# Projection products spread over attention steps by kind of step: seven shares off the diagonal, four on it

## The reference

```python
h = rmsnorm(x, a_norm)
q, k, v, g = split(h @ w_in, 4)                # w_in: 1024 x 4096
# per head, scale = 1/sqrt(64), strictly causal (s < t):
z = q @ k.T * scale
log_rem = where(mask, log_sigmoid(-z), 0)
after = reverse_cumsum(log_rem) - log_rem      # sum over s < j < t
w = where(mask, exp(log_sigmoid(z) + after), 0)
o = w @ v
y = x + (o * silu(g)) @ w_out
out = rmsnorm(y, final_norm)
```

## Time and profile before

| | |
|---|---|
| median of 3 runs | 1675.85 us (1675.66 to 1677.42) |
| profiled execution, its own time | 1678.26 us |
| its span, first to last instruction | 1676.5 us |
| mean granted TensorE clock | 0.998 |
| busy: PE, PEld, DVE, ACT, POOL | 98%, 82%, 80%, 54%, 14% |
| steps 0 to 599 | 227.8 to 1410.2 us |
| steps 600 to 639 (the last head) | 1410.2 to 1493.3 us |
| chain that ended last | PE 82%, DVE 6%, DMA 5% |

### The profile page before, as it was taken

One profiled execution on the slowest core, in us unless ns is written; L12 is line 12 of the kernel. 1 busy time (PEld: TensorE's weight loads), 2 busy tenths in 40 slices (PEclk: granted clock), 3 DMA queues, 4 the chain that ended last, 5 costly groups with the idle time before them and its releaser, 6 DMA issues.

```text
span 1676.5 us, 23300 instructions
## 1 busy us (share of the span) xinstructions
PE 1650.4 (98%) x8600; PEld 1376.7 (82%) x8600; DVE 1341.2 (80%) x1885; ACT 906.3 (54%) x1779; POOL 234.4 (14%) x212
## 2 busy tenths in 40 slices
PE   8999999999999999999999999999999999999998
PEld 6888878888888888888888888888888888778786
DVE  5435478888898989888888988898889888956765
ACT  6635255655565565656565655666565556651122
POOL 0020012110211011201110211011201110008400
PEclk9999999999999999999999999999999999999999
DMA  9958534252524243334333342425243335398632
GB/s 303 285 153 274 187 120 142 85 151 66 155 75 131 90 127 106 97 102 125 111 91 113 102 138 64 145 76 145 80 122 108 113 95 166 118 357 265 227 141 108
DMA packets 164225, 237.09 MB, mean 141 GB/s; under 512 B 49936, under 2 KB 91920, under 8 KB 164112
## 3 DMA queue, kind: packets, MB, share of 16 engines
q1 hardware_dynamic: 94624, 160.03, 30.4%
q10 hardware_dynamic: 69488, 75.58, 15.1%
HBM read 155.78 MB, written 79.76 MB: 140 GB/s over the span
## 4 chain that ended last, share of the span: by engine, by line
PE 82%; DVE 6%; DMA 5%; ACT 2%; issue 2%; POOL 1%; SPq 1%; ACTq 0%; DVEq 0%
PE proj_ps L737 27%; PE turn_ps L764 13%; PE z_ps L755 7%; PE z_ps L754 7%; PE o_ps L778 7%; PE o_ps L779 7%; PE proj_ps L692 5%; PE o_ps L692 3%; PE turn_ps L692 3%; PE turn_ps L808 2%; DMA gate<-gate_cols 1%; PE z_ps L808 1%; DVE u L1155 1%; DMA wo_raw<-in_w_out 1%; POOL w_raw L668 1%
## 5 line engine op out<-in xcount | busy, mean ns | idle before, releaser
L930 ACT ACTIVATE u<-z_ps 128x512 f32<-128x512 f32 (+3 forms) x640 | 341.8, 534 | 411.0 <-PE z_ps L755 407.5
L1155 DVE TENSOR_TENSOR_SCAN u<-u,u 128x512 f32<-128x512 f32 x384 | 491.0, 1279 | 0.0
L1160 DVE TENSOR_TENSOR r_turned_lo<-turn_ps,r_turned_hi 128x512 fp32r<-128x512 f32 (+3 forms) x640 | 376.5, 588 | 34.8 <-ACT r_turned_hi L936 33.0
L936 ACT ACTIVATE r_turned_hi<-turn_ps 128x512 fp32r<-128x512 f32 (+3 forms) x640 | 340.2, 532 | 60.0 <-issue 44.1
L668 POOL TENSOR_SCALAR w_raw<-w_raw,a_norm_col 128x128 f32<-128x128 f32 x192 | 177.0, 940 | 1202.7 <-DMA w_raw<-in_w_qkg 1202.7
L764 PE MATMUL turn_ps<-ident,u 128*128 128x128 f32 x2176 | 343.1, 273 | 0.1
L737 PE MATMUL proj_ps<-hT_hi,w_hi 128*128 128x512 f32 x768 | 320.2, 417 | 0.0
L737 PE MATMUL proj_ps<-hT_lo,w_hi 128*128 128x512 f32 x768 | 320.0, 417 | 0.0
L737 PE MATMUL proj_ps<-hT_hi,w_lo 128*128 128x512 f32 x768 | 319.8, 416 | 0.0
L764 PEld LDWEIGHTS turn_ps<-ident,u 128*128 128x128 f32 x2176 | 267.8, 140 | 59.3 <-DVE u L1155 0.5
L778 PE MATMUL o_ps<-r_turned_hi,dv_head 128*128 128x512 f32 (+3 forms) x640 | 231.8, 362 | 7.3 <-DVE r_turned_lo L1160 3.1
(11 more groups left out here) (122 smaller groups left out, 1647.8 us busy)
## 6 DMA issues: line engine op xcount, KB each, us to landing
qk_hi_cols<-made_hi ACTq DMA_DIRECT2D x64, 256.0 KB, 2.7
qk_lo_cols<-made_lo ACTq DMA_DIRECT2D x64, 256.0 KB, 3.2
x_T<-in_xT SPq DMA_DIRECT2D x30, 512.0 KB, 5.9
w_raw<-in_w_qkg SPq DMA_DIRECT2D x24, 512.0 KB, 3.4
x_rows<-in_x SPq DMA_DIRECT2D x16, 512.0 KB, 4.6
v_rows<-v_stage ACTq DMA_DIRECT2D x32, 256.0 KB
v_here<-v_rows SPq DMA_DIRECT2D x64, 128.0 KB, 3.1
v_next<-v_rows SPq DMA_DIRECT2D x64, 128.0 KB, 3.2
```

The source lines that it names most:

```text
L930: nc.scalar.activation(u_t[(m // CB) % RU][STEPS[m][3]][:, 0:w], z_ps[m % RZ][:, 0:w], ACT.Sigmoid, scale=-Z_SCALE).then_inc(s_u, 1)
L936: nc.scalar.activation(rt_hi[m % RT][:, 0:w], t_ps[m % RT][:, 0:w], ACT.Copy).then_inc(s_hi, 1)
L1155: nc.vector.tensor_tensor_scan(u, u, other, start, ALU.mult, op).then_inc(s_r, 1)
L1160: nc.vector.tensor_tensor(rt_lo[m % RT][:, 0:w], t_ps[m % RT][:, 0:w], as_f32(rt_hi[m % RT][:, 0:w]), ALU.subtract).then_inc(s_lo, 1)
```

## The change

The products per step are no longer the same for every step. Each off-diagonal step has 7 shares, each diagonal step 4, and a share is 0.5825 product; `SHARES` is the running sum. The totals stay: the last step with products is 636 in both. Steps in which groups end move by up to two; `SHORT_FROM` becomes 603 and the first three of `PIECE_STEP` 607, 611, 615; `WO_FROM` and what lies behind it stay.

```diff
-FILL_NUM, FILL_DEN = 677, 200
+SHARE_WHOLE, SHARE_DIAGONAL = 7, 4
+FILL_NUM, FILL_DEN = 5825, 10000
+
+
+SHARES = [0]
+for _, c, j, _ in STEPS:
+    SHARES.append(SHARES[-1] + (SHARE_DIAGONAL if j == c else SHARE_WHOLE))
 
 
 def filled(n):
 
     made = BEFORE * QPM + LEAD_FILL * min(n + 1 + LEAD_SCORES, LEAD_SCORES)
-    return min(made + max(n + 1, 0) * FILL_NUM // FILL_DEN, NG * QPM)
+    return min(made + SHARES[min(max(n + 1, 0), NS)] * FILL_NUM // FILL_DEN, NG * QPM)
```

## The result

The changed kernel takes 1689.17 us (median of 4 runs, 1688.37 to 1692.47) against 1675.76 for the kernel before in the same comparison: ratio 1.0086, 95% interval [1.0074, 1.0097]. The forecast was 1675.2 in a range of 1669.5 to 1681.5. It was wrong in direction and outside its range; the slower rival (1682.9) had the sign and half of the size.

A forecast was written before the change was run, and what follows sets the result against it. The prediction took TensorE (PE) to bound the kernel. Its terms, +2.1 - 2.2 - 0.5 = -0.6 us against the profiled 1678.26, with the runs' median 2.4 lower, gave 1675.2 us, range 1669.5 to 1681.5.

The forecast's parts named there:

- the slower rival: VectorE runs out at each head's start and in the third chunk, 0.5 us in 30 places: 1682.9 us, chance 0.15.
- What bounds the kernel: TensorE bounds both kinds of step; 5.3 us of real stall in steps 0 to 599, 3.3 in the last head.
- Products: Per-step products shift between diagonal and off-diagonal steps; their total (2304), last step (636) and PE's busy time stay.
- DVE's lead: Steps 0 to 599: shorter diagonal steps eat VectorE's lead; 7.4 us of stall replaces 5.3, net +2.1 us.
- the upper bound of +9.7: Steps 0 to 599: 30 places, two a head, at 0.5 us each, less the 5.3 us of old stall.
- Queues and waits moved: Weight loads, scaling and halves move one or two steps: 0 us, bounds -1 and +1.
- The evacuation of o_ps: In a chunk's first step it ends 0.5 to 0.6 us before weigh and loses 0.24: still covered, 0.
- The last head: Later output-stage loads and pieces meet longer steps; stall falls from 3.3 to 1.1 us: -2.2, bounds -3.3 and 0.
- the last three steps, 636 to 639: After step 622 the w_out loads hold the time, and two later products lie under that: 0 us.
- Clock: Rival: the granted clock falls to the lower level in the 15 third-chunk stretches, +90 us, chance 0.01.
- Nothing: Rival: the change does nothing because PE's instructions are the same, 1675.9 us, inside the forecast's band of chance 0.59.
- the stalls go: Rival: VectorE's lead is larger than assumed, 1.5 us of stall left before step 622, 1668.3 us; chance 0.25.

The follow-up runs named there:

- e4: The kernel before with made_low issued behind lo and the halves of loaded weight tiles one iteration later: ratio to before 0.9967, steps 0 to 599 in 1177.0 us.
- e11: Shares 6 off the diagonal and 7 on it, made_low behind lo, o stores behind made_high: ratio to the kernel before 0.9955, median 1667.53 us.
- e1: The changed kernel with made_low issued behind lo instead of ahead of the scan: ratio to the kernel before 0.9992, steps 0 to 599 in 1183.8 us.
- e2: The changed kernel with the halves of loaded weight tiles made one iteration later: ratio to the kernel before 1.0059, steps 0 to 599 in 1192.1 us.
- e5: The kernel before with made_low behind lo alone: ratio to before 0.9965, steps 0 to 599 in 1179.0 us.

## Why the prediction was wrong, point by point

**What bounds the kernel: right.** PE's instruction stream is the floor, and what can be won or lost is stall. A stretch without stall is 1177 us (e4, e11), against 1182.4 before: 5.4 us, where I had worked out 5.3.

**Products: right.** Their count and PE's time for them stayed. Four products fewer stand before step 600 (0.9 us), which I had not counted, since they were to be given back later.

**DVE's lead, the step that failed.** It said: "It falls below zero in 18 places [...] and the largest shortfalls of these places sum to 7.4 us", net +2.1. By the same working the stall was 18.1 us, net +12.8, beyond even the upper bound of +9.7. Two things in that step were off.
- The step took 0.23 us off each lead for every product lost since the PE instruction that last released VectorE, and left the way from there alone. But that way goes through ScalarE, where the made half stands behind the o_ps evacuation, a sigmoid that waits for PE's scores, two store issues and hi, and then through VectorE's made_low, scan and lo. I had the row for it, 64.7 us in 49 waits, and read it as a thing that keeps the lead from growing. It is what makes the lead short. Of the 19 steps before step 600 whose lead was under 0.25 us before, 16 had a wait for a made half as VectorE's last wait of over 0.1 us (13 of them over 0.15 us, the least that the views show); in the changed kernel it is 27 of 35, by either limit. A tally by the wait would have shown that most tight places are of one kind.
- The groups end in other steps after, and I used their old ones. Where made_low fell in positions 18 and 30 the lead was 0.05 to 0.45 already, with nothing left to take 0.24 to 0.5 from; elsewhere it lands on a lead that I had counted as safe: steps 98 and 190 had leads of 2.70 and 1.86 us before and, with made_low now in them, 0.06 and 0.05 after.

**The slower rival: its sign right, its mechanism half right.** It put the stalls at a head's start and in the third chunk, at 0.5 us in 30 places, because full-width scans meet short steps there. PE's weight loads waited in 38 places, in the second chunk and right behind it too (steps 57, 98, 220, 418, 419, 539), and a stall was up to 2.1 us. The sign that the prediction had set for this rival, a wait for L1160 above 13 us, was met: 18.6. e1 shows that the scans are not the cause: with them unchanged and only made_low moved, 13.2 of the stretch's 14.6 us are gone. What was right in it is the short step.

**Queues and waits moved: undersized.** I put 0 with bounds of -1 and +1 for the weight halves; e2 took 4.5 us off the changed kernel. Part of that cost was there before (the same move took 2.0 us off the stretch from e5 to e4, and nothing by the ratio), so what the change added is less than 4.5 and not measured by itself. I had looked at whether ScalarE would wait for GpSimd, and not at what a late w_hi does to VectorE, where w_lo (1.22 us) stands ahead of the next scan and lo. The evacuation of o_ps was as said: its wait went from 0.4 to 1.0 us.

**The last head: the direction right, part of the gain from elsewhere.** -2.2 was forecast, -3.6 measured. Where it was forecast, between the weighs of steps 605 and 611, 15.8 us became 13.4. VectorE's wait for gate_cols before its first piece fell from 2.55 to 1.0 us (1.6 forecast):

```profile
DVE o_part_hi L1176 <- DMA gate<-gate_cols: 1.0, 1, 1.0
```

Between steps 599 and 605 it was 0.7 less and between 611 and 636 it was 1.0 more. The remaining 1.6 us fell in the last three steps, 636 to 639, for which the prediction had put 0. First these steps before, then after, then a stretch of the output stage after:

```profile
1486.30:1493.30 7.00, 7.00 (x26) 5.67 (x27) 1.27 (x4) 1.04 (x3) 0.00 (x0) 0.76 1.06 366
```
```profile
1497.50:1502.90 5.40, 5.40 (x26) 4.51 (x27) 1.24 (x4) 1.04 (x3) 0.00 (x0) 1.00 0.93 299
1568.80:1572.30 3.50, 3.50 (x10) 2.74 (x9) 1.84 (x8) 1.35 (x3) 0.00 (x0) 0.51 1.10 351
```

The instructions of the three steps are the same. Before, the granted clock fell to the lower level at 1486.3 us for some 3.5 us, behind a wait of 2.04 us of PE for the evacuation of o_ps. After, that wait was 0.96 us and the clock stayed at 1.00; it fell later, at 1568.8, behind a wait of 3.1 us in the output stage. So these 1.6 us were moved and not won: what follows the last head took 2.1 us longer, and the head and the end together gave 1.5. No experiment separates the small rest.

**Clock: right for steps 0 to 599, a row overlooked for the last head.** The granted clock is 1.00 in the stretch before and after, so the rival didn't happen. But "no row shows a fall" isn't so: the earlier trace rows has 0.98 for the last head, the stretch at the lower level just shown.

**Nothing, and the stalls go: didn't happen.** Less stall off the diagonal brought nothing, since nearly all of it had been on and behind diagonal steps before too.

## What to carry to other kernels

Ahead of spreading filler unevenly, list the tight places by the wait that made each of them tight, and follow that wait through every in-order queue it passes: a wait of the helper work (here 2.85 us for a half that nobody needed soon) costs little where steps are long and much where they are short. Put helper work that waits behind the work that the bounding engine needs next; that one move was worth 5.9 us with the even spread and 15.8 with the uneven one, and left 4.5 of the 13.4 us between the two spreads. A subtraction of mean step lengths can't see any of this: of the stretches in the earlier trace rows VectorE was 92% busy at most, and only 78 to 79% in the diagonal ones, the kind of step in which it was late. And look up the granted clock of each stretch that is compared: here 1.6 us of a gain was a short piece at the lower level that came elsewhere.

## What the runs showed that I had not expected

Idle time of VectorE that moves from one instruction to another can be free or dear by place alone: 100 us of it (70.6 and 29.5) stood ahead of made_low in the changed kernel; in e1 there were 110.8 us ahead of lo instead, and the stretch was 13.2 us shorter. And the price of a short step is uneven: 0.32 products more on a diagonal step took 0.8 us off the stretch, 0.31 fewer added 4.7, 1.06 fewer 14.6.
